# A decoder step with 64 experts: another order of the gathered token rows, and the combine weights computed one step later

## The reference

```python
def moe_ffn(h, p):
    b, s, d = h.shape
    t = h.reshape(b * s, d)
    scores = jax.nn.sigmoid((t @ p['w_router']).astype(jnp.float32))
    ...
    _, e_idx = lax.top_k(jnp.where(e_mask, biased, -jnp.inf), TOP_K)
    w = jnp.take_along_axis(scores, e_idx, axis=-1)
    w = w / jnp.sum(w, axis=-1, keepdims=True) * ROUTE_SCALE
    combine = jnp.einsum('tk,tke->te', w, jax.nn.one_hot(e_idx, N_EXPERTS, dtype=jnp.float32)).astype(h.dtype)
    gte = jnp.einsum('td,edf->tef', t, p['w_gate_e'])
    upe = jnp.einsum('td,edf->tef', t, p['w_up_e'])
    routed = jnp.einsum('tef,efd->td', jax.nn.silu(gte) * upe * combine[:, :, None], p['w_down_e'])
    shared = (jax.nn.silu(t @ p['w_gate_s']) * (t @ p['w_up_s'])) @ p['w_down_s']
    return (routed + shared).reshape(b, s, d)
```

## Time and profile before

| | us |
|---|---|
| three runs | 963.48, 965.28, 965.52 |
| their median | 965.28 |
| the profiled execution | 965.52 |
| its span, first to last instruction | 963.1 |
| expert block, within the span | 474.7 to 963.1 |
| PE busy | 902.5 |
| DVE busy | 328.6 |

### The profile page before, as it was taken

One profiled execution on the slowest core, in us unless ns is written; L12 is line 12 of the kernel. 1 busy time (PEld: TensorE's weight loads), 2 busy tenths in 40 slices (PEclk: granted clock), 3 DMA queues, 4 the chain that ended last, 5 costly groups with the idle time before them and its releaser, 6 DMA issues.

```text
span 963.1 us, 18238 instructions
## 1 busy us (share of the span) xinstructions
PE 902.5 (94%) x7483; PEld 560.8 (58%) x7483; DVE 328.6 (34%) x822; ACT 197.3 (20%) x489; POOL 154.1 (16%) x185
## 2 busy tenths in 40 slices
PE   4899999998898888989899999999999999999996
PEld 3688888876555557845755544554454455455442
DVE  0423670037343498616422322211222222222214
ACT  1100101226222169215111111111111111111102
POOL 0000000023376000000122121221212212112110
PEclk9999999999999899999999999999999999999999
DMA  9876575627599375997699999999999999999992
GB/s 371 330 291 278 195 302 211 262 68 273 163 344 343 142 297 192 377 430 300 266 425 419 416 422 420 421 419 421 421 420 419 424 419 422 421 416 425 418 412 102
DMA packets 58917, 325.46 MB, mean 338 GB/s; under 512 B 16178, under 2 KB 25251, under 8 KB 37651
## 3 DMA queue, kind: packets, MB, share of 16 engines
q1 hardware_dynamic: 44930, 305.54, 78.4%
q0 software_dynamic: 12176, 18.56, 5.7%
q10 hardware_dynamic: 1728, 0.18, 0.1%
HBM read 326.65 MB, written 15.81 MB: 356 GB/s over the span
## 4 chain that ended last, share of the span: by engine, by line
PE 42%; DMA 7%; DVE 1%; ACT 0%; issue 0%; DVEq 0%
PE bank L2235 21%; PE bank L2175 10%; DMA done_out<-in_w_e 7%; PE bank L2186 6%; PE bank L2153 3%; PE bank L2267 1%; PE bank L2221 1%; DVE slot_b L2559 0%; DVE slot_b L2567 0%; PE bank L2205 0%; PE bank L2213 0%; DVE hh L2461 0%; ACT sge L2358 0%; ACT slot_b L2375 0%; ACT xt L2349 0%
## 5 line engine op out<-in xcount | busy, mean ns | idle before, releaser
L368 PE MATMUL bank<-h,ring 128*128 128x264 f32 x672 | 154.6, 391 | 2.9 <-DMA ring<-in_w_units 2.3
L368 PEld LDWEIGHTS bank<-h,ring 128*128 128x128 f32 x672 | 127.8, 192 | 27.0 <-issue 3.0
L2358 ACT ACTIVATE sge<-bank 64x256 f32<-64x256 f32 x64 | 24.1, 377 | 396.1 <-PE bank L2235 396.1
L2461 DVE TENSOR_TENSOR hh<-sge,bank 64x256 f32<-64x256 f32 x64 | 27.1, 423 | 223.2 <-ACT sge L2358 223.2
L2235 PE MATMUL bank<-done_out,xt 128*64 128x256 f32 x832 | 95.5, 382 | 1.7 <-DMA done_out<-in_w_e 1.7
L2235 PE MATMUL bank<-ring,xt 128*64 128x256 f32 x800 | 91.8, 382 | 1.1 <-DMA ring<-in_w_e 0.8
L1563 POOL DMA_INDIRECT xg<-tok_rows,tab_g x32 | 32.0, 999 | 331.7 <-PE bank L2153 319.3
L2401 DVE COPY sq<-bank 128x512 f32<-128x512 f32 x64 | 44.3, 692 | 103.3 <-PE bank L2175 95.1
L2175 PE MATMUL bank<-ring,ht 128*32 128x512 f32 x320 | 76.4, 598 | 0.3 <-DMA x<-in_w_e 0.3
L2235 PEld LDWEIGHTS bank<-done_out,xt 128*64 128x64 f32 x832 | 57.9, 137 | 29.5 <-DMA done_out<-in_w_e 2.0
L2186 PE MATMUL bank<-sq,wmat 64*128 64x512 f32 x256 | 71.9, 640 | 0.0
(11 more groups left out here) (478 smaller groups left out, 1217.2 us busy)
## 6 DMA issues: line engine op xcount, KB each, us to landing
ring<-in_w_units SPq DMA_DIRECT2D x28, 2048.0 KB, 10.7
done_out<-in_w_e SPq DMA_DIRECT2D x26, 2048.0 KB
ring<-in_w_e SPq DMA_DIRECT2D x25, 2048.0 KB
slot_b<-in_w_e SPq DMA_DIRECT2D x13, 2048.0 KB
ring<-in_w_e SPq DMA_DIRECT2D x20, 1024.0 KB
slot_b<-in_w_e SPq DMA_DIRECT2D x11, 1024.0 KB
done_out<-in_w_e SPq DMA_DIRECT2D x11, 1024.0 KB
row_of<-in_w_e SPq DMA_DIRECT2D x11, 1024.0 KB
```

What stands on the lines that cost most here:

```text
L368: mm = pe.matmul(bank[:, t % NB, 0:T], w[:, j, k, :], h[:, k, :], start=(k == 0), stop=(k == KD - 1))
L2358: act.activation(sg[e % 2][:, :], bank[0:LB, 4, 0:FE], ACT.Silu).then_inc(sg_ready, 1)
L2461: dve.tensor_tensor(hh[e % 2][:, :], sg[e % 2][:, :], bank[LB:2 * LB, 4, 0:FE], ALU.mult).then_inc(hh_ready, 1)
```

## The change

It has two parts.

1. The places get another order. Rank r = 4a + b, with b in 0 to 3 and a in 0 to 7, now goes to place 8b + a. Line 1920 writes it, and the copy to `ht` (now L2468) undoes it. As many elements are copied by as many instructions; the access patterns of the copy are 4 x 4 x 8 in place of 4 x 8 x 4.
2. `weights()` is called in DVE's step e = 0, behind the product `hh` of expert 0, and no more ahead of the loop.

```diff
-for i in range(4): ins = dve.tensor_scalar(listed_p[:, i * HB:(i + 1) * HB].rearrange("p (c d) -> p d c", d=4),
-                                           listed_f[:, :].rearrange("p (d c) -> p d c", d=4),
+for i in range(4): ins = dve.tensor_scalar(listed_p[:, i * HB:(i + 1) * HB].rearrange("p (b a) -> p a b", b=4),
+                                           listed_f[:, :].rearrange("p (a b) -> p a b", b=4),
...
-                        weights()
                         for e in range(NE):
                             dve.wait_ge(sg_ready, e + 1)
                             if e >= 2:
                                 dve.wait_ge(ht_done, e - 1)
                             dve.tensor_tensor(hh[e % 2][:, :], sg[e % 2][:, :], bank[LB:2 * LB, 4, 0:FE], ALU.mult).then_inc(hh_ready, 1)
+                            if e == 0:
+                                weights()
                             if e >= 2:
                                 half_out(e - 2, 6)
                             dve.wait_ge(ht_done, e + 1)
                             if e >= 4:
                                 dve.wait_ge(half_done, 2 * (e // 2 - 1))
-                            dve.tensor_copy(ht[e % 4][:, :, :].rearrange("p k n -> p (k n)").rearrange("p (x d c) -> p x c d", x=4, d=4),
-                                            bank[:, 7, 0:2 * LB].rearrange("p (x c d) -> p x c d", x=4, d=4)).then_inc(ht_ready, 1)
+                            dve.tensor_copy(ht[e % 4][:, :, :].rearrange("p k c -> p (k c)").rearrange("p (x a b) -> p x b a", x=4, b=4),
+                                            bank[:, 7, 0:2 * LB].rearrange("p (x b a) -> p x b a", x=4, b=4)).then_inc(ht_ready, 1)
```

More of the change, by code:

```diff
@@ L1919, in take_lists @@
                                     for i in range(4):
-                                        ins = dve.tensor_scalar(listed_p[:, i * HB:(i + 1) * HB].rearrange("p (c d) -> p d c", d=4),
-                                                                listed_f[:, :].rearrange("p (d c) -> p d c", d=4),
+                                        ins = dve.tensor_scalar(listed_p[:, i * HB:(i + 1) * HB].rearrange("p (b a) -> p a b", b=4),
+                                                                listed_f[:, :].rearrange("p (a b) -> p a b", b=4),
                                                                 ccol("side")[:, 2 * (i % 2) + i // 2:2 * (i % 2) + i // 2 + 1],
```

## The result

The changed kernel takes 978.08 us (median of 7 runs, 972.56 to 980.69) against 965.52 us for the kernel before (median of 7 runs, 961.58 to 968.24). The ratio is 1.0122, with a 95% interval of 1.0092 to 1.0153: it is slower by 8.9 to 14.8 us. The prediction was 976.2 us, range 972.5 to 979.5.

The account below looks back on a forecast made before the run. The DMA engine that finishes last was taken to set the end. From the profiled 965.5 us, +10.9 for the order and 0 for the later `weights` gave 976.4; against the median, 976.2 us, range 972.5 to 979.5.

Parts of the forecast that it names:

- What bounds the kernel: Expert stage: full DMA engines set the end, one to one; PE delays under its 4.4 us of waits are hidden.
- Who carries the rows: Gathers: every second DMA engine gets nearly all real rows, its neighbour almost none; the busiest goes from 125 to 198.
- (a): Gather places: each DMA engine serves four neighbouring places of one list and the same four of the next; +10.9 us.
- (b): Rival on gather places: each DMA engine serves eight neighbouring places; faster, 963.3 us; chance 0.07.
- The size: Gathers on the most loaded DMA engine: 73 more rows at 0.150 us each, +10.9 us if it finishes last.
- its bounds (8.3 to 12.6): Stage end, in us: 8.3 if an odd engine is last now, up to 12.6 by the even engines' gains.
- Part 2: `weights` behind the first `hh`: POOL's chain 6.0 us later, PE stands 2.4 us at `combine(0)`, hidden; 0 on the end.
- the DMA engines do not notice: During PE's early 2.4 us stall, the DMA queue is several us deep, so 0 on the end.
- The copies: Line 1920 and the copy to `ht`: other strides cost or give some 0.1 us once for the lists, nothing for `ht`.
- The signs: Profile after: weight waits from near expert 45, 11 to 15 us; last step near 952; DMA share under 1, about 400 GB/s.

Follow-up runs that it names:

- experiment 1: New order of the places alone, `weights()` back ahead of the loop, against the kernel before: 976.76 us, ratio 1.0111.
- 4: No permutation, rank r in place r with plain copies, against the kernel before: 981.98 us, ratio 1.0159.
- experiment 5: Order of before, but unused places read a row too, 240 rows on each DMA engine, against the kernel before: 986.7 us, ratio 1.0234.
- experiment 2: Later `weights()` alone, with the order of the places of before, against the kernel before: 964.90 us, ratio 1.0006.
- experiment 3: Second list of each expert mirrored, 83 to 100 rows per DMA engine, against the kernel before: 963.75 us, ratio 0.9987.
- 6: Both lists of each expert mirrored, counts of before (64 to 125) on mirrored engines, against the kernel before: 967.27 us, ratio 1.0034.

## Why the prediction was right, point by point

**What bounds the kernel: right.** The DMA engines set the end. Where the last ones get more to do, the stage grows nearly one to one (experiments 1, 4, 5); where PE alone is held up, nothing happens (2); without the gathers PE sets the end, 3.3 us earlier.

**Who carries the rows: right.** The reading (a) of the earlier trace rows, four neighbouring places of one list and four of the next, foretold an alternation of full and empty engines. The profile after shows half of the engines at work in the last slices, and the landing signals fall into two groups of eight with 17 us between them. Under (b) the change would have been a gain of 2 us.

**The size: right in the sum, weaker in its reason.** 10.9 us were forecast for part 1; the stage grew by 10.3 us with the order alone and 10.7 us with both parts. But I took the value of the engine that goes from 125 to 198 rows, on the assumption that it is last. Experiments 3, 5 and 6 speak against that for the kernel before: the late engines had fewer rows. The forecast held since in the changed kernel all the even engines gain about the same, 70 to 84 rows, so that it mattered little which one was last, as its bounds (8.3 to 12.6) said. That 10.9 was hit within 0.6 us is in part luck. Why some engines are late without rows isn't settled. The instruction fetches of the earlier trace rows are a candidate; no run told them from an engine that is slower by itself.

**Part 2: right that it is hidden, too small in the stall.** `weights` itself ran as foretold behind the first `hh`. The chain through POOL moved, and DVE stood for it at the matrix of pair 0:

```profile
477.82 0.42 DVE L2460 TENSOR_TENSOR hh<-sge,bank 64x256 f32<-64x256 f32 x1 [5.82 <-ACT sge L2358]
...
480.06 0.58 DVE L2415 TENSOR_SCALAR wgt<-wgt,need 128x64 f32<-128x64 f32 x3
480.68 0.40 DVE L2468 COPY ht<-bank 128x128 f32<-128x128 f32 x1
...
498.46 0.35 DVE L2434 TENSOR_SCALAR wmat<-comb,tok_f,tok_j 128x128 f32<-128x128 f32 x1 [7.74 <-DMA tok_j<-weight_tab,tok_i]
```

PE waited 3.0 us for it at `combine(0)` and, in the step of expert 4, 0.9 us for the gather of pair 3. The forecast had 2.4 us and no second wait. Two steps were off. The first gather of weights was issued 4.6 us later against the start of the stage (490.46 less 473.70; before, 488.22 less 476.09), not 6.0, but from its issue to the matrix it took 8.0 us in place of 6.0; so the matrix came 6.6 us later. (POOL's line in the changed kernel:)

```profile
490.46 1.07 POOL L2104 DMA_INDIRECT tok_j<-weight_tab,tok_i  x1 [7.81 <-DMA weight_tab<-wgt]
```

And the gather of token rows queued behind was said to move too, but its lateness was not added up. In experiment 2 the two waits together were 2.4 us. All of it stays under the 4.4 us of the earlier trace rows.

That "the DMA engines do not notice" holds only for the end. In the changed kernel some of them ran dry behind the stall:

```profile
510.00:520.00 10.00, 10.00 (x85) 5.20 (x84) 2.09 (x6) 1.55 (x4) 2.93 (x3) 1.00 0.89 349
```

In this stretch experiment 1, with the same order and no stall, has a share of 1.01 and 422 GB/s, and experiment 2, with the stall and the order of before, 1.01 and 414. The stage of the changed kernel is only 0.4 us longer than that of experiment 1, so this idle time did not reach the end. That it fell on the engines with few rows is likely but not shown, since the view doesn't name the engines.

**The copies: right.** The copy to `ht` takes 0.390 us where it took 0.383, line 1920 0.253 where it took 0.250, and nothing waits for them.

**The signs: mostly right.** PE's waits for weights begin at expert 47 (I said near 45), the last step at 949.6, with a stage that began 2.4 us earlier (I said near 952), and the DMA share falls to 0.83; the rate falls to 340 GB/s, further than the 400 that I gave. The sum of the waits is 7.7 us, less than the 11 to 15 that I gave: 3.9 us of lateness came as the early stall, and 3.3 us as slower matmuls (below). The sign in POOL's queue, three or four real rows in a row on one engine, can't be read, since the view doesn't name the engine of a packet.

## What to carry to other kernels

A gather of single rows is shared out over the DMA engines by the place of each row in the destination, so unused places should be spread over all sets of places that one engine serves, and the sets should be read from a trace, not assumed. When the DMA engines are full through a stage, count the work per engine: a mean share of 1 with a good total rate does not show that one of them is the last. A stall of an engine that runs ahead of full DMA engines costs nothing until its lead is gone. By the same reasoning a gain there should bring nothing either, which no run tested.

## What the runs showed of the hardware that I had not expected

A wait of 2.16 us for weights at 854 us was followed by a step of 32 matmuls that took 5.32 us, where all its neighbours take 3.67; the same happened at 903.48 us, with 5.36. The granted clock of these stretches is 0.98 and 0.97, where before it was 1.00. The step itself, and what follows it, show a short stay at the lower level of 1.2 GHz:

```profile
856.18:861.50 5.32, 5.32 (x33) 3.01 (x34) 0.00 (x0) 0.00 (x0) 0.00 (x0) 0.68 1.00 420
861.50:865.00 3.50, 3.50 (x27) 1.34 (x26) 1.11 (x2) 0.96 (x2) 1.84 (x2) 1.00 1.03 426
```

So each of these two waits cost PE another 1.7 us. The length of the wait alone does not decide it: the second of them was 1.72 us long, while in experiment 1 a wait of 1.80 us (before 921.02 us) was followed by a step of 3.67 us. The lost time seems hidden here, since the next wait in the chain is again for a weight DMA; no run tested it.

The DMA engines are not alike even with like counts. With 240 rows on each (experiment 5) the first was done with the last gate and up weights 7.8 us before the last, and with 83 to 100 rows on each (experiment 3) 8.1 us before.
